# Two layer heads and the retention state's copy in a hybrid retention and attention trunk: work moved between and within engine queues

## The reference

```
h = rmsnorm(x, norm1_g)
q_r,k_r,v_r,g_r, q_d,k_d,v_d, ga,gb = split(h @ w_in)         # projections
q_d = rope(rmsnorm(q_d, q_norm_g)); k_d = rope(rmsnorm(k_d, k_norm_g))   # norm per head of 64
lam = exp(sum(lq1*lk1)) - exp(sum(lq2*lk2)) + lam_init
a = softmax(q1 k1) - lam * softmax(q2 k2); o_d = a @ v_d      # 8 heads, block-causal
S_new = S * g_len + (k_r * zeta)^T v_r                        # 4 retention heads; S is an output
o_r = (decayed q_r k_r^T) v_r + (q_r S) xi ; rmsnorm(o_r)
```

## Time and profile before

| | us |
|---|---|
| median of 3 runs | 2244.57 |
| lowest, highest | 2242.88, 2245.14 |
| the profiled execution | 2245.43 |
| its span, first to last instruction | 2243.5 |

### The profile page before, as it was taken

One profiled execution on the slowest core, in us unless ns is written; L12 is line 12 of the kernel. 1 busy time (PEld: TensorE's weight loads), 2 busy tenths in 40 slices (PEclk: granted clock), 3 DMA queues, 4 the chain that ended last, 5 costly groups with the idle time before them and its releaser, 6 DMA issues.

```text
span 2243.5 us, 43652 instructions
## 1 busy us (share of the span) xinstructions
PE 2206.9 (98%) x17792; PEld 2097.3 (93%) x17792; DVE 1217.1 (54%) x2106; ACT 993.4 (44%) x1916; POOL 857.9 (38%) x378
## 2 busy tenths in 40 slices
PE   6999999999999999999999999999999999999998
PEld 6899889999999999999988889899899999999998
DVE  5676665555455553256255766565563556523553
ACT  4554554444323442344245555544452234424443
POOL 4244323334344443443443343232243434434433
PEclk9999999999999999999999999999999999999999
DMA  4232222221222222321322232222222222222222
GB/s 165 68 110 76 91 75 88 81 94 63 76 81 90 92 72 79 107 95 59 104 90 73 86 103 83 71 88 69 88 80 76 80 91 89 71 93 98 95 66 98
DMA packets 82231, 193.73 MB, mean 86 GB/s; under 512 B 7569, under 2 KB 36593, under 8 KB 82033
## 3 DMA queue, kind: packets, MB, share of 16 engines
q1 hardware_dynamic: 60272, 173.50, 23.6%
q10 hardware_dynamic: 21760, 17.45, 2.4%
HBM read 177.50 MB, written 13.42 MB: 85 GB/s over the span
## 4 chain that ended last, share of the span: by engine, by line
PE 94%; ACT 2%; DVE 1%; issue 1%; POOL 0%; DMA 0%; ACTq 0%; DVEq 0%; POOLq 0%
PE ps L627 14%; PE ps L629 14%; PE ps L628 14%; PE ps L678 7%; PE ps L679 6%; PE ps L680 6%; PE ps L1046 4%; PE ps L1045 4%; PE ps L1047 4%; PE ps L701 2%; PE ps L779 2%; PE ps L811 2%; PE ps L846 2%; PE ps L657 2%; PE ps L771 1%; PE ps L781 1%
## 5 line engine op out<-in xcount | busy, mean ns | idle before, releaser
L505 POOL TENSOR_TENSOR wlo<-raw,whi 128x1024 fp32r<-128x1024 f32 (+1 forms) x330 | 769.3, 2352 | 1061.6 <-ACT whi L1109 1061.6
L627 PE MATMUL ps<-hl,whi 128*128 128x272 f32 x2432 | 704.4, 290 | 0.0
L629 PE MATMUL ps<-hl,wlo 128*128 128x272 f32 x2432 | 701.9, 289 | 0.0
L628 PE MATMUL ps<-hl,whi 128*128 128x272 f32 x2432 | 700.5, 288 | 0.0
L627 PEld LDWEIGHTS ps<-hl,whi 128*128 128x128 f32 x2432 | 459.2, 189 | 1.5
L629 PEld LDWEIGHTS ps<-hl,wlo 128*128 128x128 f32 x2432 | 458.2, 188 | 0.0
L628 PEld LDWEIGHTS ps<-hl,whi 128*128 128x128 f32 x2432 | 457.7, 188 | 0.0
L1109 ACT ACTIVATE whi<-raw 128x1024 fp32r<-128x1024 f32 (+1 forms) x330 | 313.3, 997 | 202.9 <-PE ps L1047 176.5
L678 PE MATMUL ps<-whi,hl 128*128 128x256 f32 x1216 | 351.1, 289 | 5.6 <-ACT rawk L1204 4.4
L679 PE MATMUL ps<-wlo,hl 128*128 128x256 f32 x1216 | 344.8, 284 | 0.0
L680 PE MATMUL ps<-whi,hl 128*128 128x256 f32 x1216 | 344.3, 283 | 0.0
(11 more groups left out here) (237 smaller groups left out, 3377.5 us busy)
## 6 DMA issues: line engine op xcount, KB each, us to landing
raw<-in_w_units_dram SPq DMA_DIRECT2D x260, 512.0 KB, 4.7
raw<-in_w_down_units_dram SPq DMA_DIRECT2D x64, 352.0 KB, 3.4
out_new_k_prompt_dram<-rawk ACTq DMA_DIRECT2D x8, 512.0 KB, 3.0
out_new_v_prompt_dram<-vd ACTq DMA_DIRECT2D x8, 512.0 KB, 3.0
raw<-in_w_first_dram SPq DMA_DIRECT2D x6, 512.0 KB, 4.7
out_y_dram<-x SPq DMA_DIRECT2D x8, 272.0 KB, 6.3
kc_n<-in_cache_k_dram SPq DMA_DIRECT2D x8, 256.0 KB, 2.9
vc_n<-in_cache_v_dram SPq DMA_DIRECT2D x8, 256.0 KB, 3.3
```

The lines of the kernel that those rows point to most:

```text
L505: e.tensor_tensor(wlo[:, s, a:b], raw[:, s, a:b], whi[:, s, a:b].bitcast(F32), ALU.subtract).then_inc(*S.up("w_ready", ("lo", j, part)))
L627: e.matmul(out, wh, hi, start=(c == 0), stop=False)
L628: e.matmul(out, wh, lo, start=False, stop=False)
L629: ins = e.matmul(out, wl, hi, start=False, stop=(c == KC - 1))
```

## The change

- Phase P: the low parts of the first query unit are made by VectorE (`first_lo`, after `norm_lo` of x chunks 1 and 3) and no longer by GpSimd. The lambda products move ahead of VectorE's sums of squares.
- Phase S: ScalarE takes the exponential of lambda right after the rounding of unit 1; VectorE does the lambda steps and `hr` ahead of the sample's sum.
- Phase D, p = 0: ScalarE copies key tile 0 and rounds the values' unit (`hi("D", 1)`) before the block of waits and the square of the queries. VectorE sums the keys' squares before it applies anything to the queries. GpSimd takes both powers one after the other and only then makes the low parts of unit 2. TensorE transposes the queries after values tile 3 (m == 3).
- All p: the keys' sums, means and powers use columns 20 to 39 of their tiles.
- Phase R: ScalarE copies the new state before it squares the running rows' outputs.

```diff
@@ pool_program
-            lo("P", 0)
@@ phase D
                     if p == 0:
                         lo("D", 1)
                         power(20, "q", sem="qk_sum")
+                        power(20, "k", at=20, sem="qk_sum")
+                        lo("D", 2)
                     else:
                         power(20, "q", sem="qk_sum")
                         lo("D", 1)
-                    lo("D", 2, (0,))
-                    power(20, "k", sem="qk_sum")
-                    lo("D", 2, (1,))
+                        lo("D", 2, (0,))
+                        power(20, "k", at=20, sem="qk_sum")
+                        lo("D", 2, (1,))
@@ pe_program, queries(m)
-                        if m == (2 if p == 0 else 1):
+                        if m == (3 if p == 0 else 1):
@@ act_program, phase S
                     hi("S", 1, 0)
                     hi("S", 1, 1)
+                    e.wait_ge(*S.at("lam_ready", k=0))
+                    e.activation(lam_exp[:, :], lam_sum[:, :], ACT.Exp)...
                     e.wait_ge(*S.at("rs_ready", "rstd"))
...
-                    e.wait_ge(*S.at("lam_ready", k=0))
-                    e.activation(lam_exp[:, :], lam_sum[:, :], ACT.Exp)...
@@ act_program, phase D
+                    def key_tile(m):
+                        e.wait_ge(*S.at("mm_ready", ("N", 0, m)))
+                        e.activation(rawk[:, m, :], pv(D_BANKS["k"][m], P, UC), ACT.Copy, scale=rs1[:, m:m + 1])...
+                    if p == 0:
+                        e.wait_ge(*S.at("kv_out", k=0))
+                        key_tile(0)
+                        hi("D", 1, 0)
+                        hi("D", 1, 1)
                     for s in ("dve_step", "dve_free_o", "kv_out", ...):
                         e.wait_ge(*S.at(s, k=0))
                     square(rawq, "q")
...
+                            if p == 0 and m == 0 and u == 0:
+                                continue
@@ act_program, phase R
-                        squares(S, e, hh, NT)
                         e.wait_ge(*S.at("s_ready", ("sfin", hh)))
...
                         e.activation(sout[:, 0, :], pv("s0", P, RET_DV), ACT.Copy)...
+                        squares(S, e, hh, NT)
@@ dve_program, phase P
+            def first_lo(part):
+                h = slice(part * UNIT // 2, (part + 1) * UNIT // 2)
+                e.wait_ge(*S.at("hi_ready", ("hi", 0, part)))
+                e.tensor_tensor(wlo[:, 0, h], raw[:, 0, h], whi[:, 0, h].bitcast(F32), ALU.subtract)...
             for c, part in CUT:
                 norm_lo(c, part, vecs[:, 0, c:c + 1])
+                if c in (1, 3):
+                    first_lo(c // 2)
             normed_samples()
-            for c, part in CUT:
-                if c and part != 0:
-                    norm_sum(c, part)
...         (the lambda products)
+            for c, part in CUT:
+                if c and part != 0:
+                    norm_sum(c, part)
@@ dve_program, phase S
                     norm_mean("mm1")
+                    layer_lambda(l)
+                    e.wait_ge(*S.at("rs_ready", "rstd"))
+                    e.tensor_scalar(hr[:, :], rs1[:, :], 0.5, None, ALU.mult)...
                     e.wait_ge(*S.at("pool_step", "zeroed"))
                     sample_sum(rawq[0:DEC, NT, :], S_BANKS[NT], ("N", 0, NT), "q")
-                    e.wait_ge(*S.at("rs_ready", "rstd"))
-                    e.tensor_scalar(hr[:, :], rs1[:, :], 0.5, None, ALU.mult)...
-                    layer_lambda(l)
@@ dve_program, phase D
                     if p == 0:
-                        qk_apply(rawq, "q", 0, between=lambda: qk_sums("k"))
+                        qk_sums("k")
+                        qk_apply(rawq, "q", 0)
```

More of the change, by code:

```diff
@@ L1169, in act_program @@
                     hi("S", 1, 1)
+                    e.wait_ge(*S.at("lam_ready", k=0))
+                    e.activation(lam_exp[:, :], lam_sum[:, :], ACT.Exp).then_inc(*S.up("act_step", key="lexp"))
                     e.wait_ge(*S.at("rs_ready", "rstd"))
@@ L1175, in act_program @@
                     rest_copy(S_BANKS[NT], ("N", 0, NT), None)
-                    e.wait_ge(*S.at("lam_ready", k=0))
-                    e.activation(lam_exp[:, :], lam_sum[:, :], ACT.Exp).then_inc(*S.up("act_step", key="lexp"))
                 for p in S.bodies("D"):
@@ L1183, in square @@
                                          *S.up("act_step", key=("sq", name)))
+                    def key_tile(m):
+                        e.wait_ge(*S.at("mm_ready", ("N", 0, m)))
+                        e.activation(rawk[:, m, :], pv(D_BANKS["k"][m], P, UC), ACT.Copy, scale=rs1[:, m:m + 1]).then_inc(
+                            *S.up(f"act_free_{D_BANKS['k'][m]}", ("k", m)))
+                    if p == 0:
[3 more added lines that the diff above has]
+                        hi("D", 1, 1)
                     for s in ("dve_step", "dve_free_o", "kv_out", "o_ready", "t_ready", "dve_free_mm1", "dve_free_s1b",
@@ L1201, in act_program @@
                                 hi("D", 1, 1)
-                            if m < NT:
+                            if u == 0 and m < NT:
+                                key_tile(m)
+                            elif m < NT:
                                 e.wait_ge(*S.at("mm_ready", ("N", u, m)))
@@ L1643, in norm_sum @@
                 e.tensor_tensor(acc[:, :], acc[:, :], sq[:, c % 2, :], ALU.add).then_inc(*S.up("acc_ready", ("acc", c)))
+            def first_lo(part):
+                h = slice(part * UNIT // 2, (part + 1) * UNIT // 2)
+                e.wait_ge(*S.at("hi_ready", ("hi", 0, part)))
+                e.tensor_tensor(wlo[:, 0, h], raw[:, 0, h], whi[:, 0, h].bitcast(F32), ALU.subtract).then_inc(
+                    *S.up("w_ready", ("lo", 0, part)))
             def normed_samples():
@@ L1715, in dve_program @@
                     norm_mean("mm1")
+                    layer_lambda(l)
+                    e.wait_ge(*S.at("rs_ready", "rstd"))
+                    e.wait_ge(*S.own())
+                    e.tensor_scalar(hr[:, :], rs1[:, :], 0.5, None, ALU.mult).then_inc(*S.up("dve_step"))
                     e.wait_ge(*S.at("pool_step", "zeroed"))
                     sample_sum(rawq[0:DEC, NT, :], S_BANKS[NT], ("N", 0, NT), "q")
-                    e.wait_ge(*S.at("rs_ready", "rstd"))
-                    e.tensor_scalar(hr[:, :], rs1[:, :], 0.5, None, ALU.mult).then_inc(*S.up("dve_step"))
-                    layer_lambda(l)
                 for p in S.bodies("D"):
@@ L1725, in qk_sums, with qk_apply @@
                     def qk_sums(name):
+                        at = 20 if name == "k" else 0
                         e.wait_ge(*S.at("act_step", ("sq", name)))
                         e.wait_ge(*S.own())
-                        e.tensor_reduce(ss[:, 0:20], prob[:, :, :].rearrange("p a b -> p (a b)")[:, 0:TILES * UC].rearrange(
+                        e.tensor_reduce(ss[:, at:at + 20], prob[:, :, :].rearrange("p a b -> p (a b)")[:, 0:TILES * UC].rearrange(
                             "p (g d) -> p g d", d=DIFF_HD), AX, ALU.add).then_inc(*S.up("qk_sum", key=("ss", name)))
-                        mean(20, DIFF_HD, name, sem="qk_sum")
-                    def qk_apply(buf, name, v, between=None):
+                        mean(20, DIFF_HD, name, at=at, sem="qk_sum")
+                    def qk_apply(buf, name, v):
                         e.wait_ge(*S.at("pool_step", ("rstd", name)))
@@ L1736, in qk_apply @@
                         e.wait_ge(*S.own())
-                        e.tensor_tensor(b3, b3, rstd[:, 0:20].unsqueeze(2).broadcast_to([P, 20, DIFF_HD]), ALU.mult).then_inc(
+                        e.tensor_tensor(b3, b3, rstd[:, 20 * v:20 * v + 20].unsqueeze(2).broadcast_to([P, 20, DIFF_HD]), ALU.mult).then_inc(
                             *S.up("dve_step"))
@@ L1741, in qk_apply @@
                             *S.up("dve_step"))
-                        if between:
-                            between()
                         b4 = buf[:, :, :].rearrange("p m (h d) -> p m h d", d=DIFF_HD)
```

## The result

The changed kernel takes 2225.44 us (median of 4 runs, 2224.97 to 2226.31) against 2244.86 for the kernel before (4 runs, 2242.88 to 2245.38): the ratio is 0.9916, with an interval of 0.9898 to 0.9933. The profiled execution has a span of 2223.7 us (before 2243.5), 19.8 less.

The account below looks back on a forecast made before the run. TensorE was taken as the bound, busy 2206.9 of 2243.5 us; layer 0's 5.0, layer 1's 6.0 and retention's 2.2 summed to 13.2 us, from 2245.0 to a forecast of 2231.8, range 2228 to 2236.5.

Parts of the forecast that it names:

- The start, layer 0: Layer 0 start: VectorE makes the first low half; key tile 0's second half comes earlier, worth 0.6 us.
- the four lambda steps: Layer 0 start: four VectorE steps of 0.3 us ahead of the sums of squares, charged with 1.2 us.
- Key tile 3: Both layer heads: copying key tile 0 early removes the waits of 3.2 and 1.2 us before key tile 3.
- The wait at the query transposes: Both layer heads: query transposes start late, by 1.7 us in layer 0 and 1.25 us in layer 1.
- Two hits on the six steps: Query rotation: two GpSimd pieces meet two of VectorE's six small steps, putting 2 x 2.37 us on the chain.
- The late sample sum of layer 0: Layer 0 head: the sum of the sample's keys comes 0.5 us later than the copy of key tile 3.
- Rival 1: Query transposes: GpSimd's unit 2 pieces miss the six steps, both transposes on time; 2.95 us more, 2228.9; chance 0.18.
- Rival 2: Query transposes, layer 0: the 1.7 us wait makes the clock fall; 2.9 us back, 2234.7; chance 0.12.
- Rival 3: Layer heads: GpSimd's key power shuts out both VectorE query products; 0.1 us gained, 2244.9; chance 0.04.
- the 1.5: Layer heads: a query product longer than 1.5 us beside GpSimd's key power would show the prediction wrong.
- The retention term: Spread opening phase M (L649): copying the state before the squares removes 1.1 us a layer, 2.2 in all.

Follow-up runs that it names:

- e6: The changed kernel with both pieces of the first low half back on GpSimd: 2227.29 us.
- e3: The changed kernel with the query transposes back behind values tile 2 in the first pair's head: 2237.35 us.
- e4: The changed kernel with key tile 0's copy and the values' weight rounding back behind ScalarE's square of the queries, first pair's head: 2230.13 us.
- e10: The changed kernel unaltered, run again as yardstick on the same chip as other runs: 2225.89 us (2225.40 to 2226.36).
- e5: The changed kernel with GpSimd's low parts of unit 2 held back until VectorE has ended the rotation of the queries: 2224.12 us.
- e1: The kernel before with only the retention edit, the state copied ahead of the squares: 5.8 us below the kernel before (interval 3.4 to 7.4).
- e9: The kernel of e5 with VectorE's sums of squares ahead of the four lambda steps again in layer 0's start: 2227.18 us.
- e2: The changed kernel with only the retention edit taken back: 14.2 us below the kernel before (interval 10.1 to 15.3).
- e7: The changed kernel with the state copy ahead of the squares only in the last retention head, taken back for heads 0 to 2: 2227.75 us.
- e8: The kernel of e7 with the two state stores of heads 0 to 2 issued behind the next head's rest copy: 2225.58 us.

## Why the prediction was wrong, step by step

**The start, layer 0: right, a little small.** First matmul at 13.0 and second half at 32.0 were forecast; they came at 13.02 and 31.87. In sum 0.76 us instead of 0.6. e6 shows how the term is made up: moving the first low half is worth about 2 us (the forecast had 1.7), and the four lambda steps ahead of the sums cost 1.3 of it (1.2). One figure was right without its reason: 1.3 us for a piece of 128x1024 does not follow "by width", which gives 0.81 x 1024 / 544 = 1.5; the piece took 1.23.

**Key tile 3: right.** No wait in either layer, clock 1.00 throughout, tiles at 2.9 us. That a long wait costs its clock too is shown by e3. e4 shows that it need not: the late copy cost 4.2 to 4.7 us there where 5.5 to 6.5 were expected.

**The wait at the query transposes: right mechanism, size off.** It was put at 1.7 and 1.25 us and came at 0.9 and 0.6; with the start's 0.16 that is 1.6 us, of which 1.3 arrived in the heads; I did not find the place of the other 0.3. Two hits on the six steps and full products were right to 0.1 us. What was mis-sized is the hit: the sum added 2.37 us each, but a step of 2.40 takes the place of one of 0.33, so a hit adds 2.07, and two of them 0.6 less. With 0.6 less, the forecast's own chain gives 1.1 and 0.65. The late sample sum of layer 0, put at 0.5 us, is there: ScalarE's square of the keys waits for it, while in layer 1 it starts 0.12 us after the copy of key tile 3. That is the 0.3 us by which the wait of layer 0 is the longer one; in e10 the two waits are 1.1 and 0.6. Rival 1 (no collision) is out by the rows above, and e5 puts its price at 1.3 to 1.7 where the forecast had 2.95.

```profile
43.10 1.27 ACT L1182 ACTIVATE prob<-rawk 128x1280 f32<-128x1280 f32 x1 [0.46 <-DVE rawk L1718]
```

Rival 2 (the clock falls in the transposes' wait) did not come about, but its condition, a wait of 1.7 us, was not met either: 0.92 us was not enough, nor 1.12 in e10. In e1 the transposes of layer 0 wait 1.57 us, and two microseconds later the clock is down. So that the clock held may in part be owed to a wait shorter than the one forecast; no run has a wait of 1.7 us at this place in the changed order.

```profile
61.00:63.00 2.00, 2.00 (x12) 2.00 (x12) 2.00 (x1) 0.00 (x0) 2.00 (x1) 0.58 0.00 0
```

**Rival 3, the key power shutting out both products, is out.** They took 1.55 and 1.49 us beside a power of 3.53; the 1.55 is a shade over the 1.5 that the prediction named as a sign against it, and far from a product held up for the power's length. The Trainium skill, SBUF — State Buffer, section Who interferes with whom, says that a VectorE instruction with two SBUF inputs contends with a GpSimd instruction that reads SBUF. For GpSimd's low parts the traces agree, in e9 down to a step on a single column (2.25 us instead of 0.16). For the power, which reads SBUF too, they do not: the products beside it stay at 1.55 and 1.49 us in both layers of the changed kernel, and there the measurement decides.

**The retention term: the step that failed.** "1.1 us a layer, 2.2 in all; for heads 0 to 2 nobody waits for s0: zero" was right on L649 (2.3) and wrong on the rest. Two things were left out. First, the clock behind the wait: the prediction had shown at key tile 3 that a wait takes 2.9 us of clock with it, and took the 1.2 us wait of layer 1 as the proof that short ones don't; it did not look at the granted clock behind L649 itself, where the profile of before has 0.50 in layer 0. That is 1.5 us, shown by e2. Second, who is behind the moved instruction in ScalarE's queue: the copy takes the two state-store triggers with it, and the next head's rest copy stands behind those. Neither the triggers nor that rest copy is in the prediction. That is 1.9 to 2.3 us, shown by e7 and e8. The term was 2.2 and measured 5.8.

**What is left over** is 1.3 us in phase D's short waits (before, up to 0.7 us at L811). They are smaller in e1 too, by about 1 us, although e1 changes nothing there, and e5 has a wait of 0.7 there again (L813). I take them for scatter between executions, not for an effect of the change; no experiment was made on them.

## What to carry to other kernels

When an instruction is moved on an in-order queue, the gain is read from what stands behind it, not from who waits for its result: list everything down to the next instruction on which another engine waits, DMA triggers included. Behind every wait of TensorE that a change removes, read the granted clock of the next few microseconds in the trace, in every layer; a wait of 1.1 us carried 1.5 us of slow matmuls with it. And where GpSimd and VectorE meet, place GpSimd's large pieces beside VectorE steps that nobody is about to wait for: here a meeting added some 2 us whether the VectorE step was long (3.72 instead of 1.49) or short (2.40 instead of 0.33), and less only where the step began late in the piece (the mean of the queries at 40.52 in the changed kernel, 0.93 instead of 0.18).

## What the runs showed of the hardware that I had not expected

The clock does not follow the length of the wait alone. It fell to 0.50 at waits of 3.2 (before, both layers; e1, layer 1), 3.9 and 3.6 (e3), 2.74 and 1.57 (e1, layer 0), and 1.1 and 1.0 us (before and e2, at the spread in layer 0). It stayed at 1.00 behind 2.70 us in e4, at the same place as e1's 2.74, behind 1.1 us at key tile 3 of layer 1 (before and e1), behind 1.3 and 1.1 us in e9 (L659), and behind 1.0 us at the spread in layer 1, in both kernels that have that wait. What TensorE does before the spread's wait is the same in both layers: the retention's last products and three pairs of 32-row matmuls. What decides is open.

A DMA trigger in ScalarE's queue takes 0.34 to 0.36 us when some 0.3 us lie between it and the one before (all sixteen state stores of the changed kernel). Issued back to back, the second takes 0.44 to 0.45, at seven of eight places in the kernel before. The eighth, the last inner boundary of layer 1, takes 1.61 there, and 1.14 in e2, 1.26 in e7 and 0.69 in e8: it is the place, not the execution. The long trigger is not ScalarE's alone. SyncE issues two weight loads (L431) at each inner boundary, 0.33 and 0.45 us. At this one its second took 1.37 in the kernel before, 0.91 in e2, 1.02 in e7 and 0.82 in e8, each time beside ScalarE's long one. In the changed kernel it took 1.32, with ScalarE's two already over. So the edit did not take the long trigger away; it moved ScalarE's two ahead of it. SyncE's queue at this boundary, before and changed:

```profile
1577.01 1.74 SPq L431 DMA_DIRECT2D raw<-in_w_units_dram  x2
```

```profile
1559.56 1.69 SPq L431 DMA_DIRECT2D raw<-in_w_units_dram  x2
```

Why triggers are long at this boundary stays open.
